# RMSNorm sums of a one-layer transformer block on one Trainium2 core: squares as the stationary operand instead of ones

## What is computed

```python
def rmsnorm(x, gain):
    xf = x.astype(jnp.float32)
    y = xf * lax.rsqrt(jnp.mean(xf * xf, axis=-1, keepdims=True) + RMS_EPS)
    return (y * gain.astype(jnp.float32)).astype(x.dtype)

def swiglu_ffn(u, w_in, w_out):
    gate, up = jnp.split(u @ w_in, 2, axis=-1)
    return (jax.nn.silu(gate) * up) @ w_out

h = h + 0.5 * swiglu_ffn(rmsnorm(h, ffn1_norm[i]), ffn1_w_in[i], ffn1_w_out[i])
u = rmsnorm(h, mix_norm[i])
h = h + stick_breaking_attention(u, sb_w_qkv[j], sb_w_o[j], valid)
h = h + 0.5 * swiglu_ffn(rmsnorm(h, ffn2_norm[i]), ffn2_w_in[i], ffn2_w_out[i])
```

## Time and profile before

| | us |
|---|---|
| median of 3 runs | 1983.55 (1982.08 to 1986.01) |
| profiled execution | 1982.76 |
| its span | 1981.0 |
| TensorE busy | 1905.3 |
| VectorE busy | 1318.2 |
| GpSimd busy | 1089.1 |
| ScalarE busy | 749.6 |
| mean granted clock of TensorE | 0.992 |

### The profile page before, as it was taken

One profiled execution on the slowest core, in us unless ns is written; L12 is line 12 of the kernel. 1 busy time (PEld: TensorE's weight loads), 2 busy tenths in 40 slices (PEclk: granted clock), 3 DMA queues, 4 the chain that ended last, 5 costly groups with the idle time before them and its releaser, 6 DMA issues. The chain is left out here.

```text
span 1981.0 us, 37412 instructions
## 1 busy us (share of the span) xinstructions
PE 1905.3 (96%) x12508; PEld 1739.0 (88%) x12508; DVE 1318.2 (67%) x1751; ACT 749.6 (38%) x1495; POOL 1089.1 (55%) x1010
## 2 busy tenths in 40 slices
PE   7899999999999999999999999999999999899997
PEld 6899999999999989999989987778877887778875
DVE  5877767676666768343389971297677767666676
ACT  5433343333222335222367762253334333322232
POOL 4456665655555645444477762355666566555560
PEclk9999999999999999999999999999999999999998
DMA  4234434355877411333232212014354435587732
GB/s 129 75 119 143 162 124 160 119 170 205 301 247 241 145 44 60 112 97 116 97 109 65 64 54 64 22 32 154 122 169 138 156 120 169 193 304 247 251 130 96
DMA packets 244612, 273.57 MB, mean 138 GB/s; under 512 B 12976, under 2 KB 176816, under 8 KB 244544
## 3 DMA queue, kind: packets, MB, share of 16 engines
q1 hardware_dynamic: 244544, 272.69, 41.8%
HBM read 179.58 MB, written 93.06 MB: 138 GB/s over the span
## 5 line engine op out<-in xcount | busy, mean ns | idle before, releaser
L1826 PE MATMUL psum<-arena 128*128 128x260 f32 (+3 forms) x3908 | 1245.7, 319 | 47.3 <-DVE scratch L1407 8.6
L1828 PE MATMUL psum<-arena 128*128 128x260 f32 (+3 forms) x3908 | 1228.6, 314 | 0.0
L1827 PE MATMUL psum<-arena 128*128 128x260 f32 (+3 forms) x3908 | 1226.2, 314 | 0.0
L1826 PEld LDWEIGHTS psum<-arena 128*128 128x128 f32 x3908 | 739.3, 189 | 106.6 <-issue 16.6
L1827 PEld LDWEIGHTS psum<-arena 128*128 128x128 f32 x3908 | 738.4, 189 | 45.5 <-issue 3.4
L1828 PEld LDWEIGHTS psum<-arena 128*128 128x128 f32 x3908 | 738.9, 189 | 43.6
L704 POOL TENSOR_TENSOR arena<-scratch,arena 128x512 fp32r<-128x512 f32 x365 | 516.4, 1440 | 409.8 <-ACT arena L952 409.8
L1407 DVE TENSOR_TENSOR scratch<-scratch,psum 128x520 f32<-128x520 f32 (+1 forms) x265 | 182.9, 690 | 247.4 <-PE psum L1828 188.1
L952 ACT ACTIVATE arena<-scratch 128x512 fp32r<-128x512 f32 x371 | 214.9, 622 | 319.1 <-DVE scratch L1410 117.2
L1410 DVE TENSOR_TENSOR scratch<-scratch 128x512 f32<-128x512 f32 x200 | 252.1, 1261 | 108.7 <-POOL arena L704 102.0
L796 POOL TENSOR_TENSOR arena<-scratch,arena 128x256 fp32r<-128x256 f32 x280 | 212.9, 780 | 180.7 <-ACT arena L1163 180.7
(11 more groups left out here) (93 smaller groups left out, 1296.1 us busy)
## 6 DMA issues: line engine op xcount, KB each, us to landing
scratch<-w_in_dram SPq DMA_DIRECT2D x88, 512.0 KB, 4.9
pairs<-scratch SPq DMA_DIRECT2D x140, 260.0 KB, 4.0
arena<-pairs SPq DMA_DIRECT2D x35, 1040.0 KB, 9.2
pairs<-scratch SPq DMA_DIRECT2D x140, 256.0 KB, 4.0
arena<-pairs SPq DMA_DIRECT2D x35, 1024.0 KB, 8.7
scratch<-w_out_dram SPq DMA_DIRECT2D x80, 256.0 KB, 3.1
qkv<-scratch SPq DMA_DIRECT2D x48, 260.0 KB, 2.1
scratch<-w_qkv_dram SPq DMA_DIRECT2D x24, 512.0 KB, 4.5
```

The costliest lines, as they stand in the source:

```text
L1826: nc.tensor.matmul(dst, wh, xh, start=start, stop=False, skip_group_check=True)
L1827: nc.tensor.matmul(dst, wh, xl, start=False, stop=False, skip_group_check=True)
L1828: return nc.tensor.matmul(dst, wl, xh, start=False, stop=stop, skip_group_check=True)
```

## The change

In all three norms the squares become the stationary operand. A half is cut into 5 pieces of 104 tokens (FFN2: 4 of 128), `SUM_TILES` and `SUM_ROWS`. For each tile of squares TensorE loads each piece as weights and moves one column of ones, so that the sums come out with tokens on the partitions, in 5 (4) columns of one bank. The matmuls of a half accumulate into columns of a bank that one matmul with a zero operand clears first. Root and reciprocal are taken of these 5 (4) columns, [104, 5] or [128, 4], and are put into `half_rstd`, a free part of `stats`. Then TensorE spreads them (`spread_half`): a column, broadcast over 128 weight columns, is multiplied with a piece of the identity, which gives the same row in all 128 partitions of the old bank; six matmuls for a half of 520 tokens, four for 512. VectorE's `rows` wait for this (`spread_out`) and are the same as before.

The spreads stand in TensorE's queue: for FFN1's first half behind the sums of the second half; for QKV's first half behind the second group of chunk 3; for FFN2's first half behind output group 11; for each second half in the plain unit, behind the first two blocks of its first group. The instructions of ScalarE and VectorE keep their places.

```diff
+SUM_TILES = (5, 5, 4)
+SUM_ROWS = tuple(half // tiles for half, tiles in zip(HALF, SUM_TILES))
...
+        half_rstd = [stats[:].rearrange("p a b -> p (a b)")[:, at:at + 5] for at in (10, 15)]
...
-                    sums = banks(n, NORM_BANKS[n][c])
-                    nc.scalar.activation(sums, sums, ACT.Sqrt, scale=1.0 / D_MODEL, bias=eps[:, 0:1])\
-                        .then_inc(root_taken, 1)
+                    size, tiles = SUM_ROWS[n], SUM_TILES[n]
+                    nc.scalar.activation(half_rstd[c][0:size, 0:tiles], psum[0:size, NORM_BANKS[n][c], 0:tiles],
+                                         ACT.Sqrt, scale=1.0 / D_MODEL, bias=eps[0:size, 0:1]).then_inc(root_taken, 1)
...
-                sums = banks(n, NORM_BANKS[n][c])
+                cols = half_rstd[c][0:SUM_ROWS[n], 0:SUM_TILES[n]]
                 dve.wait_ge(root_taken, 2 * n + c + 1)
-                nc.vector.reciprocal(sums, sums).then_inc(rstd, 1)
+                nc.vector.reciprocal(cols, cols).then_inc(rstd, 1)
...
-                dve.wait_ge(rstd, 2 * n + c + 1)
+                dve.wait_ge(spread_out, 2 * n + c + 1)
...
-                    half, parts_of = HALF[n], UNIT_CHUNKS[n]
-                    cols = half // parts_of
-                    for j in range(parts_of):
-                        last = nc.tensor.matmul(psum[:, bank + j, 0:cols], ones[:],
-                                                sq_half[n][m % 2][:, j * cols:(j + 1) * cols],
-                                                start=at == 0, stop=at == KT - 1)
+                    size, tiles = SUM_ROWS[n], SUM_TILES[n]
+                    if at == 0:
+
+                        nc.tensor.matmul(psum[0:size, bank, 0:tiles], ones[0:P // 2, 0:size], ident[0:P // 2, P // 2:P // 2 + tiles],
+                                         start=True, stop=False, skip_group_check=True)
+                    for j in range(tiles):
+                        last = nc.tensor.matmul(psum[0:size, bank, j:j + 1], sq_half[n][m % 2][:, j * size:(j + 1) * size],
+                                                ones[:, 0:1], start=False, stop=at == KT - 1, skip_group_check=True)
                     last.then_inc(summed, 1)
+
+            def spread_half(n, c):
+
+                pe.wait_ge(rstd, 2 * n + c + 1)
+                size, cols = SUM_ROWS[n], HALF[n] // UNIT_CHUNKS[n]
+                for j in range(UNIT_CHUNKS[n]):
+                    begin = j * cols
+                    for tile in range(begin // size, (begin + cols - 1) // size + 1):
+                        at, end = max(begin, tile * size), min(begin + cols, (tile + 1) * size)
+                        last = nc.tensor.matmul(psum[:, NORM_BANKS[n][c] + j, at - begin:end - begin],
+                                                half_rstd[c][0:size, tile:tile + 1].to_broadcast([size, P]),
+                                                ident[0:size, at - tile * size:end - tile * size], start=True, stop=True)
+                last.then_inc(spread_out, 1)
...
+                            if i == 0 and k == 1:
+                                spread_half(n, 1)
...
+                        if (c, dt) == (3, 1):
+                            spread_half(QKV, 0)
...
+                if c == 1:
+                    spread_half(FFN1, 0)
...
+                if n == KT + 3:
+                    spread_half(FFN2, 0)
```

More of the change, by code:

```diff
@@ L363, in build @@
         squared, summed, root_taken, rstd = sem("squared"), sem("summed"), sem("root_taken"), sem("rstd")
+        spread_out = sem("spread_out")
         norms = [{name: sem(f"norm{n}_{name}") for name in ("un", "hi", "lo", "lo_pool")} for n in range(3)]
```

## The result

The changed kernel took 2016.1 us (median of 4 runs, 2010.5 to 2024.8) against 1983.9 for the kernel before: a ratio of 1.0167, 95% interval 1.0144 to 1.0190, slower by 32 us. The forecast of 1993.0 had the sign, not the size; the range ended at 2014. The first rival, the falling clock, had been priced at about 2013.

A forecast was written before the change was run, and what follows sets the result against it. TensorE, busy 96% of the span, was taken to bound the kernel; FFN1 3.3, QKV 2.5 and FFN2 3.8 sum to 9.6 us, 1992.4 for the profiled execution, 1993.0 for the median. Eight-in-ten range: 1987 to 2014.

The forecast's parts named there:

- The first rival: All three norms: granted clock falls to half in long runs of one-column sums; 20 us more, about 2013; chance 0.35.
- What bounds the kernel: Whole kernel: TensorE, busy 96% of the span; time off other engines pays only where TensorE waits for it.
- FFN1's second half: FFN1's norm: the second half's reciprocal lies on VectorE's chain to TensorE, worth 3.3 us.
- QKV's first: QKV's norm, first half: TensorE idles 2.0 us for VectorE's additions behind the reciprocal, and that idling goes.
- Only one of the six stands before a wait of TensorE: All norms: of six reciprocals, 20.4 us of VectorE in all, only one precedes a TensorE wait.
- The price of a pass: New sums: one weight load with its matmul costs its load, 0.098 us for 104 columns, 0.120 for 128.
- rival 2: New sums: loads and one-column matmuls don't overlap, 0.04 us more per pass, about 2007; chance 0.10.
- rival 3: New sums: a pass costs only 0.062 us, as in the 16-column transposes, making the kernel faster, 1975; chance 0.07.
- The sum at clock 1.00: All three norms without a clock fall: 3.3 + 2.5 + 3.8 = 9.6 us slower, 1993.0; chance 0.43.
- The stall row: Old profile after the stall at 79: clock fell to 0.50 after mostly real idling, so whether loads count stayed open.
- The place of FFN1's first spread: FFN1: spread queued behind both halves' sums, so VectorE's first rows move from 29.11 to 36.5; within the +3.3.
- QKV's waits: QKV: the 1.66 us wait goes; VectorE's 3.3 us gain ends in ScalarE's 2.24 wait for a product; +2.5 paid.

The follow-up runs named there:

- the wide kernel: Changed kernel with each load of squares moving 102 columns of ones (128 in the third norm) instead of one: 1995.9 us, ratio 1.0054.

## Why the prediction was wrong

**What bounds the kernel, and that the reciprocals are worth little: right.** 4.8 us alone, against 5.3 by the forecast's steps (3.3 of FFN1's second half, 2.0 of QKV's first). That the totals are so close is luck: in the trace QKV's step gave 1.9, FFN1's 0.4 and not 3.3. The forecast let VectorE's chain decide when TensorE goes on in FFN1. With that chain some 3 us earlier, GpSimd's low parts decided, and in the changed kernel's executions TensorE, once it had its first product, waited for nothing over 0.3 us until 94.7 in one and 90.8 in the other. "Only one of the six stands before a wait of TensorE" was nearer to it.

**The price of a pass: right in kind, a little high.** Taken 0.098 and 0.120; measured at full clock 0.093 (81 passes in 7.50 us with the wide columns), and in FFN2 a tile 0.03 longer than before where 0.09 was forecast. Loads do hide their matmuls, so rival 2 is out, and nothing near 0.062 is seen, so rival 3 is out. The figure of the Trainium skill (TensorE: Matmul & The Clock Gate, section LDWEIGHTS), 0.087 for 104 columns (an estimate by its 1.2 columns a nanosecond), lies about as far below this measurement as the scaled 0.098 above it.

**The sum at clock 1.00: right, in part by luck.** 1993.0 was forecast (its terms make 1993.2); the wide kernel less its clearings stands at about 1991. By norm it has 4.7, 2.3 and 2.7 for 3.3, 2.5 and 3.8: FFN2 was priced too high for its passes, and FFN1's 4.7 hold two stretches of 3.4 us at half clock.

**The failed step: the choice among the rivals.** The forecast took the clock for 1.00 and gave the clock's fall 0.35. The argument against it was that TensorE "is never without an instruction". The trace after has exactly that, 13.20 busy of 13.20 us, at half clock. The stall row couldn't tell whether a load alone counts, as the prediction said; it should have followed that both cases were open and not that the cheaper one was likelier. The rival's 20 us held up well. Taking the wide kernel's column from the changed kernel's two, FFN1 was given 14 and had 12.8 and 10.5, QKV was given 5.2 and had 5.0 and 9.2, FFN2 was given 0.9 and had 1.5 twice: 19 and 21. The medians say 25, so the norms of two executions don't hold all of it. Measured against 2013, the rival missed by 3.

**The range was too short above.** It ended at 2014, inside the rival's own case, because I gave that case no spread: at half clock the loads of squares start 173 ns apart instead of 92, and the length of the low stretches varies from run to run (2007 to 2025 over both measurements).

**The place of FFN1's first spread: right in direction.** It was named and priced in the 3.3. VectorE's rows start 13 us earlier when it is moved up (51.23 to 38.27), but TensorE gains only 0.5 to 3 us by the traces.

**QKV's waits: right.** The wait of 1.66 us is gone after the change, and ScalarE's wait for the first product, 2.24 before, is 2.24 again at 795.63 in the changed kernel:

```profile
795.63 0.60 ACT L991 ACTIVATE scratch<-psum 128x520 f32<-128x520 f32 x1 [2.24 <-PE psum L1836]
```

TensorE still sets that meeting, and what VectorE saved in QKV's second half ended there.

## What to carry to other kernels

A reduction over partitions by matmul costs its loads once the data is the stationary operand. Count passes times the load, and don't take the vanished columns for a gain. Before giving TensorE a long run of loads with hardly a moved column, put dense products between them or price the run at half clock; a busy share of 100% in the profile was no protection here. And ask first which engine ends the stage: 19 us off VectorE were worth 5 at most, while a cheaper format for the same sums on TensorE was worth 22.

## What the runs showed of the hardware

- A run of fp32 loads, each with one moved column, let the granted clock fall to 0.50 (1.2 GHz) though TensorE was never idle; with 52 columns per load it fell too in FFN1, with 102 the first row of sums stayed at 1.00 (81 passes in 7.50 us). The Trainium skill (TensorE: Matmul & The Clock Gate, Part 1) lets the clock follow how busy TensorE has been. In these rows the profile had TensorE busy for 13.20 of 13.20 us while the clock was low, so its busy share there doesn't tell the clock.
- Making the same loads move 102 or 128 columns instead of one took 20 us off the program. It did not always keep the clock up: one execution of such a kernel had 10.2 us at half clock in FFN1's second row of sums.
- With nothing but loads of squares in the queue, a load of 104 columns starts every 92 ns at full clock, whether one column is moved or 102, and every 173 ns at half clock.
- A small root, 104x5 from PSUM, takes 262 ns and a reciprocal of 104x5 181 ns, against 657 and 3398 for the full rows.
